# Diagonals, means and the own norm placed anew around the layer norms of a two-block layer on one Trainium2 core

## The chip, the cores and the metric

One core of a Trainium2 chip runs the whole program. The metric is device microseconds of one execution. TensorE is called PE, VectorE DVE, ScalarE ACT, GpSimd POOL and SyncE, which issues the DMAs, SP.

## What is computed

x is 1024 tokens by 1024 features. A first block (gated linear attention, cross attention, an output product) is followed by a second one, of which the change touches the conformer convolution and what stands beside it:

```python
hl = modulate(rms_norm_2(xl, norm1_g[i]), sh1_l, s1_l)
yl = conformer_conv(hl, rows, *conv_p)
xl = xl + g1_l * yl
xl = xl + g2_l * sq_relu_mlp(modulate(rms_norm_2(xl, norm2_g[i]), sh2_l, s2_l), mlp_w1[i], mlp_w2[i])
...
def conformer_conv(h, n_seg, w_pw1, b_pw1, w_dw, b_dw, ln_g, ln_b, w_pw2, b_pw2):
    u = h @ w_pw1 + b_pw1
    a, gate = jnp.split(u, 2, axis=-1)
    u = a * jax.nn.sigmoid(gate)
    u = dwconv(u.reshape(B * n_seg, L // n_seg, D), w_dw).reshape(B, L, D) + b_dw
    u = jax.nn.silu(layer_norm(u, ln_g, ln_b))
    return u @ w_pw2 + b_pw2
```

The convolution is depthwise with 31 taps in segments of 64 tokens. The first block ends in an rms norm of its own (`final_norm_w`), whose result is the xl above.

## The kernel before

Features lie on partitions (8 tiles f or k of 128), tokens along the free dimension, in two halves h of 512. Every product is done in three matmuls per k and 512 tokens (weights high x data high, high x low, low x high, line 1133), called a group here; a product of 1024 inputs for one f and one h has 8 groups. Weights come as units of 128 x 1024 into a ring of four slots: SP loads a unit, ACT (line 1507) makes its high part WH, POOL (line 2320) its low part WL.

`make_plan` (line 143) writes one order of pieces, by a small model of time: `tick` advances PE's time at each group and lets lanes of DVE and POOL work run until they are `AHEAD` (2.5 us) ahead of it, and lets background generators (`bg`) take a step. Each engine's program then walks through the plan and issues, in that order, what its piece means for it; each engine works strictly in order and waits on semaphores.

Half by half the second block does this. `between_blocks(h)` makes the norms and the modulated input (`m1_mul`, `m1_hi`, `m1_lo`, the tile HB). For each f the products `pa(f,h)` and `pg(f,h)` are gated (`glu`: ACT's sigmoid at line 1714, DVE's product into a padded tile UP). Then comes the convolution: on DVE for six of the f (`tap` x 31 into the banks 4 and 5, `taps_end`, result CO for half 0, COB for half 1), for f 1 and 5 on ACT and POOL (`ptap`, lines 1738 and 2362). There are ten UP tiles, so the products of half 1 run up to f 7 while half 0 is convolved.

The layer norm of a half is `means` (a matmul of ones with each CO[f], line 1390, added up over f in one bank), then `normed`: `ysub` on DVE (CO less the mean), `ysq` on ACT (the square, tile YT), `ysum` on PE (four matmuls with one column of ones, each in two passes, line 1398), `ln_r` (DVE, POOL's power, DVE's diagonal LNDG), `ln_row` (a matmul that spreads the diagonal over the partitions, line 1373), and `z_mul`, `z_hi`, `z_lo`, the input of the second pointwise product `pw2`. The own norm of the first block is `own_norm(h)`: the diagonal DGR (DVE, line 2170), the row from it (PE, line 1373), and `pre` (DVE line 2179, ACT line 1722) for eight f, on the residual RES. `pw2` outputs are added to RES, which is why `pre(f,h)` must be done by then.

Half 0's layer norm stands alone (`beside(normed(0), ...)`): nothing else is there for PE. Half 1's (`conv_norm(1)`) runs as background beside the first groups of the MLP of half 0. After `pw2` of half 0 follow its squares (`sq`, `sq_add`, tile ACC), `n3_sum`, `n3_row`, the modulation `m2_*` and the MLP (`hid`, `w2_out`).

Of the kernel before, what the change touches and what calls it, by code (L numbers as in the profile page):

```python
# [142 lines left out]
def make_plan():  # L143
# [8 lines left out]
    hi_by = ["act"]  # L152
# [463 lines left out]
    co_done = set()  # L616
    rate[0] = 1.0

    def conv_dve(f, h):
        for k in range(TAPS):  # L620
            piece("tap", f, h, k)
            yield
        piece("taps_end", f, h)
        co_done.add((f, h))
        up_free[(8 * h + f) % 10] = True
        yield

    def conv_pool(f, h):
        piece("ptap0", f, h)
        for k in range(1, TAPS):  # L630
            piece("ptap", f, h, k)
            yield
        co_done.add((f, h))
        up_free[(8 * h + f) % 10] = True
# [26 lines left out]
    def means(h):  # L661
        take(S, "mean", h)
        for f in range(8):
            while (f, h) not in co_done:
                yield
            piece("mean", f, h)
            now["pe"] += 4 * PASS
            yield

    def normed(h):  # L670
        take(S, "ysum", h)
        for f in range(8):
# [4 lines left out]
            yield  # L677
        piece("ysum", 7, h)
# [24 lines left out]
    for h in range(2):  # L703
        for f in range(8):
# [3 lines left out]
            product("pa", f, h)  # L708
            product("pg", f, h)
# [25 lines left out]
    beside(normed(0), {7: 3, 8: 1, 9: 2, 10: 1})  # L735
# [6 lines left out]
    def second_product(h):  # L742
# [128 lines left out]
def build_program(nc, wall, wmod, xT, memT, vecs, gup, ident_d, masks_d, out, oscr):  # L871
    es = ExitStack()
    with es:
# [142 lines left out]
        YT = [[at(f"YT{h}{i}", 512, F32, x0 + (10, 18)[h] * K2 + i * K2) for i in range(2)] for h in range(2)]  # L1016
        LNDG = [at(f"LNDG{h}", 512, F32, x0 + (12, 20)[h] * K2) for h in range(2)]
# [75 lines left out]
        def pe_program(pe):  # L1093
# [409 lines left out]
        def act_program(ac):  # L1503
# [236 lines left out]
            def ysq(f, h):  # L1740
# [56 lines left out]
        def dve_program(dv):  # L1797
# [367 lines left out]
            def r1_row(h):  # L2165
# [4 lines left out]
                tt(*spread_of(DGR[:, :], hs(R1, h), 4), ALU.mult).then_inc(sig["r1_row"], 1)  # L2170
# [98 lines left out]
            def final(h, k):  # L2269
# [12 lines left out]
                        r1_row=r1_row, pre=pre, ysub=ysub, ln_r=ln_r, z_mul=z_mul, z_lo=z_lo, gbv=gbv, a2=a2, pw2=pw2, n3_sum=n3_sum, n3_row=n3_row, hid=hid,  # L2282
# [272 lines left out]
```

## Time and profile before

| | us |
|---|---|
| runs | 2236.50, 2244.32, 2230.09; median 2236.5 |
| profiled execution | 2237.09 |
| its span in the profile | 2235.3 |
| PE busy | 2081.1 (93%) |
| DVE busy | 1185.3 (53%) |
| ACT busy | 676.6 (30%) |
| POOL busy | 867.3 (39%) |

The convolution of half 0 with its products runs from about 1144 to 1345 us of the span, the layer norm of half 0 from 1345 to 1379, `pw2` and the norm behind it to 1445, the MLP of half 0 with the convolution of half 1 beside it to about 1623. Busy time is that of the data paths; an engine that waits on a semaphore is idle. The idle time given with a row is what stood before it, and the name behind the arrow is who ended it.

### The profile page before, as it was taken

What the parts mean: (1) busy time and instruction counts of PE and PEld (TensorE: products, weight loads), DVE (VectorE), ACT (ScalarE), POOL (GpSimd) and SP (SyncE); (2) the same over time, 40 slices, a digit from 0 to 9 for tenths busy, and PEclk for the clock granted to TensorE, in tenths of its full rate; (3) what the DMA queues carried; (4) which work ended last, traced back from release to release, by engine and by line L of the source; (5) the groups of instructions that cost most, each with busy time, mean ns of one, the idle gap of its engine ahead of it and who ended that gap; (6) DMA issues with size and microseconds to landing.
All of it is one profiled execution on the core that took longest, in us unless ns stands there. A gap on an engine that the chain in (4) does not pass through costs nothing.

```text
span 2235.3 us, 26278 instructions
## 1 busy us (share of the span) xinstructions
PE 2081.1 (93%) x10286; PEld 1730.9 (77%) x10286; DVE 1185.3 (53%) x1977; ACT 676.6 (30%) x1200; POOL 867.3 (39%) x511
## 2 busy tenths in 40 slices
PE   6899999898998989999979977879999999999997
PEld 5779988787887768888858766658778888888886
DVE  5353455365463346776677967979735222222226
ACT  2313222211136411010345435465434322212111
POOL 7342122221111344453438872679444442222120
PEclk9999999999899999999989997889999999999998
DMA  4211011101010454454113221123223332111112
GB/s 160 67 48 57 29 39 57 38 34 35 27 34 34 140 193 157 149 183 140 40 46 97 93 67 47 57 66 94 72 89 95 94 96 65 57 48 53 51 48 76
DMA packets 57323, 171.59 MB, mean 77 GB/s; under 512 B 6368, under 2 KB 6752, under 8 KB 57072
## 3 DMA queue, kind: packets, MB, share of 16 engines
q1 hardware_dynamic: 57200, 169.91, 23.4%
q8 instruction: 82, 1.34, 0.2%
q14 instruction: 41, 0.34, 0.0%
HBM read 157.30 MB, written 12.58 MB: 76 GB/s over the span
## 4 chain that ended last, share of the span: by engine, by line
PE 78%; DVE 11%; issue 4%; ACT 4%; POOL 2%; DMA 1%; SPq 0%; POOLq 0%; DVEq 0%; ACTq 0%
PE B L1133 37%; PE B L1316 22%; PE B L1199 6%; PE B L1237 4%; DVE B L1804 3%; DVE OSB L1807 1%; DMA MODRAW<-wmod 1%; POOL WL L2320 1%; DVE HB L1804 1%; PE B L1261 1%; DVE ACC L1801 1%; PE B L1264 1%; PE B L1398 1%; PE B L1277 1%; PE B L1373 1%
## 5 line engine op out<-in xcount | busy, mean ns | idle before, releaser
L1133 PE MATMUL B<-HB,WH 128*128 128x512 f32 x2976 | 947.2, 406 | 29.3 <-ACT WH L1507 13.5
L2320 POOL TENSOR_TENSOR WL<-RAW,WH 128x1024 fp32r<-128x1024 f32 x217 | 529.0, 2441 | 531.8 <-ACT WH L1507 525.4
L1133 PEld LDWEIGHTS B<-HB,WH 128*128 128x128 f32 x2976 | 558.8, 192 | 158.6 <-issue 32.3
L1133 PE MATMUL B<-HB,WL 128*128 128x512 f32 x1488 | 569.1, 396 | 7.2 <-POOL WL L2320 7.2
L1133 PEld LDWEIGHTS B<-HB,WL 128*128 128x128 f32 x1488 | 285.0, 192 | 71.1 <-POOL WL L2320 10.1
L1804 DVE SCALAR_TENSOR_TENSOR B<-UP,vec,B 128x512 f32<-128x512 f32 x336 | 226.6, 748 | 0.0
L1804 DVE SCALAR_TENSOR_TENSOR RES<-B,modv,RES 128x512 f32<-128x512 f32 x144 | 104.9, 747 | 195.2 <-PE B L1316 164.9
L1507 ACT ACTIVATE WH<-RAW 128x1024 fp32r<-128x1024 f32 x144 | 150.7, 1053 | 161.9 <-DMA RAW<-wall 161.9
L2318 POOL TENSOR_SCALAR WH<-RAW 128x1024 fp32r<-128x1024 f32 x73 | 85.5, 1171 | 286.6 <-DMA RAW<-wall 286.6
L2297 POOL TENSOR_TENSOR small<-small 128x4 f32<-128x4 f32 (+2 forms) x36 | 36.7, 1019 | 403.3 <-DVE small L1807 403.2
L1316 PE MATMUL B<-HIDH,WH 128*128 128x512 f32 x512 | 185.3, 395 | 0.0
L1316 PE MATMUL B<-HIDL,WH 128*128 128x512 f32 x512 | 182.9, 390 | 0.0
L1316 PE MATMUL B<-HIDH,WL 128*128 128x512 f32 x512 | 182.8, 390 | 0.0
L1199 PE MATMUL B<-WH,HB 128*128 128x256 f32 x768 | 147.4, 293 | 0.0
L1804 DVE SCALAR_TENSOR_TENSOR B<-B,RL 128x512 f32<-128x512 f32 x64 | 44.5, 696 | 190.0 <-ACT RL L1774 189.8
L1199 PEld LDWEIGHTS B<-WH,HB 128*128 128x128 f32 x768 | 122.5, 194 | 3.1 <-issue 1.5
L1804 DVE SCALAR_TENSOR_TENSOR MACC<-MODRAW,small,MACC 128x512 f32<-128x512 f32 x84 | 102.3, 1218 | 35.3 <-DMA MODRAW<-wmod 29.8
L1316 PEld LDWEIGHTS B<-HIDL,WH 128*128 128x128 f32 x512 | 96.6, 189 | 20.4 <-issue 0.7
L1316 PEld LDWEIGHTS B<-HIDH,WH 128*128 128x128 f32 x512 | 96.6, 189 | 20.3 <-issue 0.7
L1316 PEld LDWEIGHTS B<-HIDH,WL 128*128 128x128 f32 x512 | 96.5, 189 | 20.2
L1199 PE MATMUL B<-WL,HB 128*128 128x256 f32 x384 | 109.4, 285 | 0.0
L1738 ACT ACTIVATE PR<-UP,vec 128x512 f32<-128x512 f32 x120 | 84.5, 723 | 53.7 <-POOL COB L2362 32.5
(235 smaller groups left out, 2734.3 us busy)
## 6 DMA issues: line engine op xcount, KB each, us to landing
RAW<-wall SPq DMA_DIRECT2D x217, 512.0 KB, 3.5
MODRAW<-wmod SPq DMA_DIRECT2D x96, 256.0 KB, 2.7
RES<-xT SPq DMA_DIRECT2D x16, 512.0 KB, 6.8
oscr<-OT SPq DMA_DIRECT2D x32, 256.0 KB, 2.0
OI<-oscr SPq DMA_DIRECT2D x16, 512.0 KB, 3.3
outT<-RES SPq DMA_DIRECT2D x16, 256.0 KB, 2.1
mraw<-memT SPq DMA_DIRECT2D x1, 1024.0 KB, 13.7
mst<-masks SPq DMA_DIRECT2D x1, 224.0 KB, 14.7
```

Source lines behind the costliest of these rows:

```text
L1133: i = pe.matmul(bank, a[:, ks], hb(part, k, h), start=k == 0 and n == 0, stop=k == 7 and n == 2)
L1199: i = pe.matmul(bank[:, tl * 256:(tl + 1) * 256], hb(part, k)[:, t * 128:(t + 1) * 128], b[:, k % 4 * 256:(k % 4 + 1) * 256], start=k == 0 ...
L1237: i = pe.matmul(bank[0:m, c % 4 * 64:c % 4 * 64 + 64], ch(k, c)[:, 0:m], odd, start=True, stop=True)
L1261: pe.matmul(bank[:, 0:dv], ch(KT_, c), vc, start=True, stop=True).then_inc(done, 1)
L1264: i = pe.matmul(bank[:, 0:dv], ch(AB, c), vc, start=True, stop=c == 0)
L1316: i = pe.matmul(bank, a[:, ks], rhs(part, h), start=k == 0 and n == 0, stop=k == 3 and n == 2)
L1507: return ac.activation(o, i, ACT.Copy, **kw)
L1738: ac.activation(seg(PR[n % 2][:, :]), tap(f, h, k), ACT.Copy, scale=wcol(f, k)).then_inc(sig["ptap_act"], 1)
L1804: return dv.scalar_tensor_tensor(out=o, in0=a, scalar=s, in1=b, op0=op0, op1=op1)
L2297: po.tensor_tensor(o, o, mhalf[:, 0:n], ALU.pow).then_inc(sig[made], 1)
L2318: po.tensor_scalar(hi, raw, 1.0, 0.0, ALU.mult, ALU.add).then_inc(sig[f"w_hi{q % NW}"], 1)
L2320: po.tensor_tensor(lo, raw, hi.bitcast(F32), ALU.subtract).then_inc(sig[f"w_lo{q % NW}"], 1)
```

## The change

1. `r1_row` is split. The diagonal is a piece of its own, `r1_dg`, and the row a later one. In half 0 the diagonal is made where it was, and the row and the eight `pre` move from the third product into `normed(0)`, between `ysum(6,0)` and `ysum(7,0)`; the row takes a bank of the ring B in place of S. In half 1 eight background steps lie between diagonal and row.
2. `means` adds the f in the order in which the model of time has them done, each only when PE's time is `LATE` (8 us) past that, or when all are done.
3. The first `pa` and `pg` are done side by side, group by group.
4. The last `pw2` of a half lets the DVE and POOL lanes run only up to PE's time (`ahead[0] = 0.0`).
5. Four tiles YT for the squares in place of two; their places in memory and those of LNDG, SQ3, TN and DG3 move.

```diff
+LATE = 8.0
...
-            while lanes[lane] and now[lane] < now["pe"] + AHEAD:
+            while lanes[lane] and now[lane] < now["pe"] + ahead[0]:
...
     def own_norm(h):
 
+        piece("r1_dg", h)
+        for _ in range(8):
+            yield
         take(S, "r1_row", h)
         piece("r1_row", h)
...
     def means(h):
+
         take(S, "mean", h)
-        for f in range(8):
-            while (f, h) not in co_done:
-                yield
-            piece("mean", f, h)
-            now["pe"] += 4 * PASS
+        left = list(range(8))
+        while left:
+            ready = [f for f in left if (f, h) in co_done and (now["pe"] > co_done[f, h] + LATE or len(co_done) == 8 + 8 * h)]
+            if ready:
+                f = min(ready, key=lambda f: co_done[f, h])
+                left.remove(f)
+                piece("mean", f, h, len(left))
+                now["pe"] += 4 * PASS
             yield
...
+        if h == 0:
+            take(B, "r1_row", 0)
+            piece("r1_row", 0)
+            for f in range(8):
+                piece("pre", f, 0)
         piece("ysum", 7, h)
...
-            product("pa", f, h)
-            product("pg", f, h)
+            if f == 0 and h == 0:
+                names = [("pa", 0, 0), ("pg", 0, 0)]
+                together(names, names)
+            else:
+                product("pa", f, h)
+                product("pg", f, h)
...
-                bg.append(own_norm(0))
+                piece("r1_dg", 0)
...
-    beside(normed(0), {7: 3, 8: 1, 9: 2, 10: 1})
+    beside(normed(0), {9: 2, 10: 1})
...
+            if f == 7:
+                ahead[0] = 0.0
             product("pw2", f, h)
             done(f)
+        ahead[0] = AHEAD
...
-                if f >= 2:
-                    w.wait_ge(sig["ysum"], nth["ysum", f - 2, h] - h)
-                ac.activation(YT[h][f % 2][:, :], CO[h][f][:, :], ACT.Square).then_inc(sig["ysq"], 1)
+                if f >= 4:
+                    w.wait_ge(sig["ysum"], nth["ysum", f - 4, h] - h)
+                ac.activation(YT[h][f % 4][:, :], CO[h][f][:, :], ACT.Square).then_inc(sig["ysq"], 1)
```

The order that comes out differs as follows. On PE, at the first groups of `pa(2,0)` (bank B0; B3 is the end of `pg(1,0)`), before:

```order
L1133 MATMUL B3<-HB_49,WL_51 128x512
L1133 MATMUL B0<-HB_49,WH_50 128x512 x2
L1133 MATMUL B0<-HB_49,WL_51 128x512
L1373 MATMUL B6<-DGR_166,ones_54 128x512
L1133 MATMUL B0<-HB_49,WH_50 128x512 x2
L1133 MATMUL B0<-HB_49,WL_51 128x512
```

and now:

```order
L1153 MATMUL B3<-HB_49,WL_51 128x512
L1153 MATMUL B0<-HB_49,WH_50 128x512 x2
L1153 MATMUL B0<-HB_49,WL_51 128x512
L1153 MATMUL B0<-HB_49,WH_50 128x512 x2
L1153 MATMUL B0<-HB_49,WL_51 128x512
L1153 MATMUL B0<-HB_49,WH_50 128x512 x2
```

The row from DGR has left the product; the groups around it are the same.

On DVE, at the end of the convolution of half 0 (UP7 is the input of f 7, UP8 that of f 0 of half 1, UP5 the gating of `(7,1)`, CO0 the first `ysub`), before:

```order
L1804 SCALAR_TENSOR_TENSOR UP5_159<-B2,vec_56,SG1_129 128x8x64
L1804 SCALAR_TENSOR_TENSOR B5<-UP7_161,vec_56,B5 128x512
L1804 SCALAR_TENSOR_TENSOR B4<-UP7_161,vec_56,B4 128x512
L1804 SCALAR_TENSOR_TENSOR B5<-UP7_161,vec_56,B5 128x512
L1804 SCALAR_TENSOR_TENSOR CO7_137<-UP7_161,vec_56,B4 128x512
L1801 TENSOR_TENSOR CO7_137<-CO7_137,B5 128x512
L1804 SCALAR_TENSOR_TENSOR CO0_130<-B7,CO0_130 128x512
```

and now:

```order
L1824 SCALAR_TENSOR_TENSOR CO7_137<-UP7_165,vec_56,B4 128x512
L1821 TENSOR_TENSOR CO7_137<-CO7_137,B5 128x512
L1827 TENSOR_SCALAR B4<-UP8_166,vec_56 128x512
L1827 TENSOR_SCALAR B5<-UP8_166,vec_56 128x512
L1824 SCALAR_TENSOR_TENSOR B4<-UP8_166,vec_56,B4 128x512
L1824 SCALAR_TENSOR_TENSOR B5<-UP8_166,vec_56,B5 128x512
L1824 SCALAR_TENSOR_TENSOR B4<-UP8_166,vec_56,B4 128x512
L1824 SCALAR_TENSOR_TENSOR UP5_163<-B2,vec_56,SG1_129 128x8x64
L1824 SCALAR_TENSOR_TENSOR CO0_130<-B6,CO0_130 128x512
```

The taps and the end of f 7 and five taps of half 1 have gone ahead of the last gating, which the first `ysub` now follows directly. On PE the last pair of products, `pa(7,1)` and `pg(7,1)`, had `mean(5)` after one group, `mean(6)` after three and `mean(7)` behind it; now it has `mean(7)` after one group and `mean(5)` after three.

On PE, at the end of the layer norm of half 0 (YT the squares, DGR the own norm's diagonal, LNDG the layer norm's), before:

```order
L1398 MATMUL B6<-ones_54,YT01_147 128x1 x4
L1398 MATMUL B6<-ones_54,YT00_146 128x1 x4
L1398 MATMUL B6<-ones_54,YT01_147 128x1 x4
L1398 MATMUL B6<-ones_54,YT00_146 128x1 x4
L1398 MATMUL B6<-ones_54,YT01_147 128x1 x4
L1373 MATMUL B7<-LNDG0_150,ones_54 128x512
L1133 MATMUL B0<-HB_49,WH_50 128x512 x2
```

and now:

```order
L1418 MATMUL B7<-ones_54,YT03_149 128x1 x4
L1418 MATMUL B7<-ones_54,YT00_146 128x1 x4
L1418 MATMUL B7<-ones_54,YT01_147 128x1 x4
L1418 MATMUL B7<-ones_54,YT02_148 128x1 x4
L1393 MATMUL B0<-DGR_170,ones_54 128x512
L1418 MATMUL B7<-ones_54,YT03_149 128x1 x4
L1393 MATMUL B6<-LNDG0_154,ones_54 128x512
L1153 MATMUL B1<-HB_49,WH_50 128x512 x2
```

The row of the own norm stands ahead of the last sum. On DVE its eight `pre` follow the last `ysub` and stand ahead of `ln_r`, whose two instructions came there behind three taps.

In `pw2` of half 0 six taps stood ahead of the last output on DVE, and two do now. In half 1 the row from DGR stood on PE behind the first group of `hid(4)`, and stands now behind the fifth of `hid(5)`, 12 groups later; the diagonal stays behind `hid(3)` on DVE. The eight `pre` of half 1 stood there around `hid(4)` and stand now around `hid(6)`.

## Rows read from the trace of the kernel before

**Rows 1.** Busy time of each engine by stretch, us; PEclk: the granted clock.

```profile
core 0: us, PE busy (x) PEld busy (x) DVE busy (x) ACT busy (x) POOL busy (x), PEclk, DMA share, GB/s
...
1168.00:1314.00 146.00, 146.00 (x634) 119.01 (x633) 122.80 (x184) 72.50 (x97) 125.86 (x78) 1.00 0.29 91
...
1348.00:1363.00 15.00, 13.79 (x64) 13.73 (x64) 6.11 (x11) 6.06 (x9) 0.39 (x1) 0.50 0.00 1
...
1500.00:1600.00 100.00, 99.09 (x445) 80.40 (x443) 86.75 (x132) 47.24 (x66) 75.57 (x44) 1.00 0.29 90
1600.00:1681.00 81.00, 77.75 (x348) 63.08 (x348) 35.67 (x51) 32.05 (x43) 31.08 (x15) 0.98 0.26 80
```

**Rows 2.** PE's waits by line and releaser: us in all, times, longest.

```profile
PE B L1373 <- DVE DGR L1801: 16.4, 2, 9.3
...
PE B L1390 <- POOL CO L2362: 11.9, 1, 11.9
PE B L1352 <- DVE ACC L1801: 8.7, 3, 5.6
```

**Rows 3.** Timeline of PE at `pa(2,0)`: start, us, operation, idle time before.

```profile
1165.96 2.05 PE L1373 MATMUL B<-DGR,ones 128*128 128x512 f32 x2 [9.34 <-DVE DGR L1801]
```

**Rows 4.** Timeline of DVE, own norm and first gatings of half 0.

```profile
1168.05 5.36 DVE L1804 SCALAR_TENSOR_TENSOR RES<-RES,vec,B 128x512 f32<-128x512 f32 x8 [2.23 <-PE B L1373]
...
1190.39 0.76 DVE L1804 SCALAR_TENSOR_TENSOR UP<-B,vec,SG 128x512 f32<-128x512 f32 x1 [5.51 <-ACT SG L1714]
1191.06 8.65 DVE L1804 SCALAR_TENSOR_TENSOR B<-UP,vec,B 128x512 f32<-128x512 f32 x13
1201.27 0.75 DVE L1804 SCALAR_TENSOR_TENSOR UP<-B,vec,SG 128x512 f32<-128x512 f32 x1 [1.56 <-ACT SG L1714]
```

**Rows 5.** Timeline of POOL: splits of weights, and the last adds of the convolution.

```profile
1165.55 2.48 POOL L2320 TENSOR_TENSOR WL<-RAW,WH 128x1024 fp32r<-128x1024 f32 x1 [12.37 <-ACT WH L1507]
...
1173.55 2.40 POOL L2320 TENSOR_TENSOR WL<-RAW,WH 128x1024 fp32r<-128x1024 f32 x1
...
1315.15 11.13 POOL L2362 TENSOR_TENSOR CO<-CO,PR 128x512 f32<-128x512 f32 x8 [1.74 <-ACT PR L1738]
```

**Rows 6.** Timeline of PE at the means of half 0.

```profile
1326.34 2.08 PE L1390 MATMUL B<-CO,ones 128*128 128x512 f32 x2 [11.93 <-POOL CO L2362]
...
1344.93 2.08 PE L1390 MATMUL B<-CO,ones 128*128 128x512 f32 x2 [4.97 <-DVE CO L1801]
```

**Rows 7.** Timeline of DVE, end of the convolution and layer norm of half 0.

```profile
1314.56 0.75 DVE L1804 SCALAR_TENSOR_TENSOR UP<-B,vec,SG 128x512 f32<-128x512 f32 x1 [0.79 <-ACT SG L1714]
...
1340.77 0.75 DVE L1804 SCALAR_TENSOR_TENSOR UP<-B,vec,SG 128x512 f32<-128x512 f32 x1 [14.92 <-issue]
...
1344.19 0.69 DVE L1801 TENSOR_TENSOR CO<-CO,B 128x512 f32<-128x512 f32 x1
1347.04 4.87 DVE L1804 SCALAR_TENSOR_TENSOR CO<-B,CO 128x512 f32<-128x512 f32 x8 [2.17 <-PE B L1390]
...
1362.37 0.16 DVE L1807 TENSOR_SCALAR small<-B 128x4 f32<-128x4 f32 x1 [8.42 <-PE B L1398]
```

**Rows 8.** Groups of PE and ACT by line, from 1348 to 1363 us.

```profile
L1398 PE MATMUL B<-ones,YT 128*128 128x1 f32 x64 | 13.8, 352 | 1.5 <-ACT YT L1751 1.5
...
L1751 ACT ACTIVATE YT<-CO 128x512 f32<-128x512 f32 x8 | 5.0, 630 | 14.0 <-DVE CO L1804 7.1 <-PE B L1398 6.9
```

**Rows 9.** Timeline of PE: a column sum of the first block's norm.

```profile
1131.65 0.95 PE L1352 MATMUL B<-ones,ACC 128*128 128x1 f32 x8
```

**Rows 10.** Timelines of DVE and PE at the end of `pw2` of half 0.

```profile
1418.62 4.03 DVE L1804 SCALAR_TENSOR_TENSOR B<-UP,vec,B 128x512 f32<-128x512 f32 x6
...
1425.64 1.87 PE L1352 MATMUL B<-ones,ACC 128*128 128x1 f32 x8 [5.65 <-DVE ACC L1801]
```

**Rows 11.** Timelines of DVE and PE at the own norm of half 1.

```profile
1471.29 0.68 DVE L1801 TENSOR_TENSOR DGR<-ident,small 128x512 f32<-128x512 f32 x1
...
1472.12 2.05 PE L1373 MATMUL B<-DGR,ones 128*128 128x512 f32 x2 [7.08 <-DVE DGR L1801]
```

More of the change, by code:

```diff
@@ L151, in make_plan @@
     lanes = {"dve": [], "pool": []}
-    hi_by = ["act"]
+    hi_by, ahead = ["act"], [AHEAD]
     def u_split():
@@ L615, in make_plan @@
     up_free = [True] * 10
-    co_done = set()
+    co_done = {}
     rate[0] = 1.0
@@ L623, in conv_dve @@
         piece("taps_end", f, h)
-        co_done.add((f, h))
+        co_done[f, h] = now["dve"]
         up_free[(8 * h + f) % 10] = True
@@ L632, in conv_pool @@
             yield
-        co_done.add((f, h))
+        co_done[f, h] = now["pool"]
         up_free[(8 * h + f) % 10] = True
@@ L1015, in build_program @@
               [at(f"COB{f}", 512, F32, hb0 + (8 + f) * K4 + K2) for f in range(8)]]
[L1016 to L1017 removed]
+        YT = [[at(f"YT{h}{i}", 512, F32, x0 + (10, 18)[h] * K2 + i * K2) for i in range(4)] for h in range(2)]
+        LNDG = [at(f"LNDG{h}", 512, F32, x0 + (14, 22)[h] * K2) for h in range(2)]
         RL = at("RL", 512, F32, x0 + 16 * K2)
@@ L1384, in r1_row, with mean @@
             def r1_row(h):
-                row(("r1_row", h), DGR[:, :], "r1_row")
-            def mean(f, h):
-                bank, done = start(("mean", h), f == 0)
+                row(("r1_row", h), DGR[:, :], "r1_dg")
+            def mean(f, h, left):
+                bank, done = start(("mean", h), left == 7)
                 conv_done(w, f, h)
-                i = pe.matmul(bank, ones[:, :], CO[h][f][:, :], start=f == 0, stop=f == 7)
-                if f == 7:
+                i = pe.matmul(bank, ones[:, :], CO[h][f][:, :], start=left == 7, stop=left == 0)
+                if left == 0:
                     i.then_inc(done, 1)
@@ L1397, in ysum @@
                 for t in range(4):
-                    i = pe.matmul(bank[:, t:t + 1], YT[h][f % 2][:, t * 128:(t + 1) * 128], ones[:, 0:1],
+                    i = pe.matmul(bank[:, t:t + 1], YT[h][f % 4][:, t * 128:(t + 1) * 128], ones[:, 0:1],
                                   start=f == 0 and t == 0, stop=f == 7, skip_group_check=True)
@@ L2163, in taps_end, with r1_dg @@
                 tt(co, co, BANKS[5], ALU.add).then_inc(sig["taps_end"], 1)
-            def r1_row(h):
+            def r1_dg(h):
                 w.wait_ge(sig["n1_pow"], 2 * h + 1)
@@ L2169, in r1_row @@
                     wait_full(w, "r1_row", 0)
-                tt(*spread_of(DGR[:, :], hs(R1, h), 4), ALU.mult).then_inc(sig["r1_row"], 1)
+                tt(*spread_of(DGR[:, :], hs(R1, h), 4), ALU.mult).then_inc(sig["r1_dg"], 1)
             def pre(f, h):
@@ L2281, in dve_program @@
                         m1_lo=m1_lo, m2_mul=m2_mul, m2_lo=m2_lo, glu=glu, tap=tap_, taps_end=taps_end,
-                        r1_row=r1_row, pre=pre, ysub=ysub, ln_r=ln_r, z_mul=z_mul, z_lo=z_lo, gbv=gbv, a2=a2, pw2=pw2, n3_sum=n3_sum, n3_row=n3_row, hid=hid,
+                        r1_dg=r1_dg, pre=pre, ysub=ysub, ln_r=ln_r, z_mul=z_mul, z_lo=z_lo, gbv=gbv, a2=a2, pw2=pw2, n3_sum=n3_sum, n3_row=n3_row, hid=hid,
                         w2_out=w2_out, n4_sum=n4_sum, n4_row=n4_row, final=final)
```

6 lines of the change are left out of this document (3 added, 3 removed).

## The prediction, made before the changed kernel was run

> **What bounds the kernel now.** I read first the busy shares, then the waits of TensorE (PE), then the timelines of its neighbours around each wait that the change touches. PE is the engine to follow: from 1168 to 1314 us it is busy without a gap, and from 1500 to 1681 us nearly so [rows 1]. So time is won only where PE stands still, and every microsecond won there moves all that follows. Its long waits near the change are few [rows 2]: 16.4 us in two waits for DGR, the diagonal of the own norm; 11.9 us for CO from GpSimd (POOL), a mean that isn't ready; and the waits for sums of squares (ACC), 5.6 us of them at the end of the second pointwise product of half 0. Besides these there is the layer norm of half 0: PE is busy in it, but with one-column matmuls at a granted clock of 0.50 [rows 1, 8], and the whole chain behind it waits.
>
> **Half 0, the row taken out of the third product (+8.4, later +7.4).** PE ended a group of `pa(2,0)` at 1156.62 and stood 9.34 us until DGR was made [rows 3]. DVE made DGR only after the whole modulation of half 1. Now the product goes on. Two products of eight groups take 1201.27 - 1190.39 = 10.88 us [rows 4], 0.68 a group. The 15 groups left of `pa(2,0)` and `pg(2,0)` end at 1156.4 + 15 x 0.68 = 1166.6. Then a new wait: the low part of the next weights is POOL's, whose split starts at 1165.55 as before, since ScalarE (ACT) reaches its half of it only behind the modulation; it is done at 1168.0, so `pa(3,0)` ends near 1173.4. The split after it comes behind four adds of the convolution and ends at 1173.55 + 2.40 = 1175.95 [rows 5]; nothing of the change moves it. So `pg(3,0)` ends at 1175.95 + 5.1 = 1181.0. Before it ended about 1.0 us ahead of the gating at 1190.39, at 1189.4. Of 10.4 us freed (the wait, and about 1.1 for the row), 8.4 are kept. From there POOL's two splits and four adds a pair (2 x 2.40 + 4 x 1.39 = 10.4 us, [rows 5]) stay below the 10.88 of PE, so the lead holds. DVE has its eight own-norm rows (5.36 us, [rows 4]) taken away and 13 to 15 taps of 0.665 us (8.65 / 13, [rows 4]) per pair: it keeps up. By the gating of `(6,1)` one more mean has been placed on PE; two passes cost 2.08 us at the low clock [rows 6], about 1.0 at the high one. So that gating moves from 1314.56 [rows 7] to 1307.2. Bounds: 4 (a third weight wait) to 10.4.
>
> `pa(0,0)` and `pg(0,0)` side by side I cost at nothing: PE then has more to do while DVE delivers k by k, but the same seven groups stand behind the sum of squares of half 1, which waits for DVE's ACC in either order. Freed slots come 10 us later for one weight load, and its split is needed only 10 us after that. Bounds -1 to +2.
>
> **Half 0, means by completion (+9.3).** Before, PE met `mean(5)` after one group of the last pair, waited 11.93 us for POOL, and the gating `(7,1)` fell at 1340.77; DVE stood 14.9 us for it with 4 taps of `(7,0)` to go, ended them at 1344.88 and subtracted the mean from 1347.04 [rows 6, 7]. Now DVE finishes `(7,0)` in front of that gating: 1307.2 + 0.7 + 10 x 0.665 + 0.7 = 1315.2. PE meets `mean(7)` near 1307 and waits 8 us for it, in place of 11.9 and 5.0. `mean(5)` is ready by then: POOL's last eight adds took 11.13 us from 1315.15 [rows 5]; seven, 7.4 us earlier, end at 1317.5. What follows the first of two means was 15.1 us before (1326.34 to the end of the gating, 1341.43; [rows 6, 7]) and consists of the same groups now. So the subtraction starts at 1330.3 in place of 1347.04: 16.7 in all, 7.4 + 9.3. The new chain is convolution, mean, product, gating, subtraction; before, the product lay beside it. Bounds 5 to 12.
>
> **Half 0, layer norm (-4.0).** Two buffers of squares never held PE: its 64 one-column matmuls run 13.79 us without a gap, 1.72 us for each f, while ACT, at 0.63 a square, waits for PE [rows 8]. Four buffers shorten nothing there. But `r1_row` now stands ahead of the last column sum on PE (2.08 us at the low clock), and DVE has eight rows of `pre` (5.36 us) queued ahead of `ln_r`. With the clock low throughout: the first sum starts 1.5 us after the subtraction, seven sums 12.0, the row 2.1, `pre` 5.4: 21.0 us from subtraction to `ln_r`, where 1362.37 - 1347.04 = 15.3 stood [rows 7]. That costs 5.7. What they hide in is only the last 1.7 us sum. If the clock stayed high, a sum would cost 0.95 (eight such matmuls at 1131.65, [rows 9]) and the total would be 1.5 + 6.6 + 1.1 + 5.4 = 14.6, a gain of 0.7. PE comes to it after ten busy microseconds and a stand of 3 us, so I let two sums run fast: -4.0. Bounds -5.7 and +0.7. ACT's eight `pre` follow DVE's one by one, and the row of the norm behind `ln_r` covers the last of them.
>
> The Trainium skill (TensorE: Matmul & The Clock Gate, Part 1, "What's actually happening") says that the throttled clock is the default and that activity releases it. Read simply, gapless PE should be given its full clock; the row at 0.50 speaks against that for one-column matmuls. By the rule the layer norm would gain 0.7 instead of losing 4.0 and the sum would be 27.2; that is rival B.
>
> **Half 0, fewer taps ahead of the last output (+2.4).** Six taps ran in front of the last `pw2` output, 1418.62 to 1422.65, while PE had ended at 1425.64 - 5.65 = 1419.99 [rows 10]. Two taps end at 1419.95. The four moved ones are made up before `hid(0)`, where DVE bounds: both orders have 23 taps from the row of n3 to there, so the 2.4 stays. Bounds 0 to 2.5.
>
> **Half 1, diagonal ahead of its row (+7.4).** PE stood 7.08 us for DGR, with one group of `hid(4)` done, and ran the row at the low clock [rows 11]. Now 12 groups lie between; DGR, made at 1471.97, is ready when the row is reached near 1475. 7.1 are saved, 1.0 more from the clock, and 0.7 given back where the mean of f 7 and the first square meet PE late. From 1500 to 1600 us DVE is busy 86.75 and POOL 75.57 of 100 us [rows 1]: following 7 us faster uses most of DVE's room, so I bound it by 1.5 (DVE becomes the bound) and 9. Behind it PE is busy to the end and nothing gives the lead back.
>
> Sum: 7.4 + 9.3 - 4.0 + 2.4 + 7.4 = 22.5. Against the profiled execution's 2237.1 (span 2235.3 and 1.8 around it) that is 2214.6; this execution is 0.6 above the median of the runs, 2236.5, from which I go: **2214.0 us**. About 1%, 22.4 us, is what a measurement of this kernel can tell from no change; the forecast sits on that line.
>
> **Rivals.**
> A, the forecast: 0.55, own range 2209 to 2219.
> B, the layer norm at the high clock: 2214.0 - 4.7 = 2209.3. For it: 0.95 us a sum after busy PE. Against: 13.79 us at 0.50. 0.08.
> C, half 1 isn't kept: DVE or POOL can't follow, and PE waits again for a bank or weights: 7.4 becomes 1.5, 2219.9. For it: DVE 87% busy. Against: 13 us in 100 are idle there [rows 1]. 0.17.
> D, the lead of the first product is eaten by weights: ACT and POOL serve splits between taps in a fixed order; 8.4 becomes 3.4: 2219.0. For it: two new waits already in my count. Against: the cadence, 10.4 below 10.88. 0.13.
> E, slower: the last product of half 0 now stands behind `mean(7)`. Should the taps of `(7,0)` end where they did (1344.88), because DVE and not PE paces them, the subtraction starts at 1344.88 + 15.1 = 1360.0, 13.0 late; with -4.0, +2.4 and +7.4 the kernel takes 7.2 more: 2243.7. It decides from an end of taps past 1315.2 + 22.5 = 1337.7. Against: DVE idled ahead of each gating shown (5.51, 1.56, 0.79 us, [rows 4, 7]). 0.07.
> That the change doesn't do what it says is open for the four buffers alone, and is in A.
>
> **How the numbers follow.** The range 2206 to 2226 takes in A with its bounds, B, C and D; E is outside. Faster by over 1% (below 2214.1): half of A's 0.55, B, and some of the upper bounds of C and D: 0.45. Slower by over 1% wants E worse than worked out, or two losses at once: 0.04. The rest, 0.51, is within 1%.
>
> **What would show it.** In the changed profile: no DGR among PE's waits; the pair of f 3 gated at about 1182; a wait of 7 to 9 us for CO7 from DVE and none from POOL; subtraction near 1330; PE's one-column run with a row in it, DVE's `ln_r` 19 to 21 us behind the first subtraction; the ACC wait near 3.2 us; no new PE wait after 1450. A first subtraction later than 1338 breaks the second term, a PE wait for weights or banks between 1460 and 1600 the last one, and a clock of 1.0 in the sums the third.

## The result: 2216.0 us, and half of the terms moved elsewhere

| | before | changed |
|---|---|---|
| median | 2241.1 us (5 runs, 2230.1 to 2244.3) | 2216.0 us (5 runs, 2214.1 to 2221.6) |
| ratio | | 0.9902, 95% interval 0.9873 to 0.9932 |
| span of the profiled execution | 2235.3 us | 2214.2 us |

The prediction said 2214.0 us, 22.5 us saved; the spans differ by 21.1, the medians by 25.1, since the two further runs of the kernel before moved its median from 2236.5 to 2241.1. The total came out, but not by the sum that was written down: one term was half due to another cause than the one named, one loss was taken too small, and one gain was won in full and then mostly lost to a wait that the prediction had not seen. The waits of the matrix engine in the changed kernel (line and releaser, us in all, times, longest):

```profile
PE B L1153 <- POOL WL L2340: 10.1, 7, 2.2
...
PE B L1410 <- DVE CO L1821: 8.3, 1, 8.3
...
PE B L1393 <- DVE LNDG L1821: 5.9, 1, 5.9
...
PE B L1153 <- issue: 4.9, 1, 4.9
...
PE B L1418 <- ACT YT L1771: 3.8, 2, 3.0
```

DGR (16.4 us in [rows 2]) is gone, and so is the mean of POOL (11.9). The wait for CO from DVE is 8.3 us, as forecast, where 5.0 stood [rows 6]; LNDG has 5.9 us, where 3.0 stood in two waits; and new are 4.9 us with "issue" as releaser: nothing that the profile could name.

DVE in half 0 (start, us, operation, idle time before it), to be laid beside [rows 4, 7]: the gating of f 3, that of `(6,1)`, the end of f 7, the last gating, the first subtraction, the eight `pre`, and `ln_r`:

```profile
1181.62 0.75 DVE L1824 SCALAR_TENSOR_TENSOR UP<-B,vec,SG 128x512 f32<-128x512 f32 x1
...
1304.52 0.75 DVE L1824 SCALAR_TENSOR_TENSOR UP<-B,vec,SG 128x512 f32<-128x512 f32 x1 [1.15 <-ACT SG L1734]
...
1311.89 0.69 DVE L1821 TENSOR_TENSOR CO<-CO,B 128x512 f32<-128x512 f32 x1
...
1327.19 0.75 DVE L1824 SCALAR_TENSOR_TENSOR UP<-B,vec,SG 128x512 f32<-128x512 f32 x1 [11.26 <-issue]
1327.86 4.86 DVE L1824 SCALAR_TENSOR_TENSOR CO<-B,CO 128x512 f32<-128x512 f32 x8
1343.30 5.36 DVE L1824 SCALAR_TENSOR_TENSOR RES<-RES,vec,B 128x512 f32<-128x512 f32 x8 [10.58 <-PE B L1393]
1348.57 0.15 DVE L1827 TENSOR_SCALAR small<-B 128x4 f32<-128x4 f32 x1
```

The gating of f 3 moved from 1190.39 to 1181.62, that of `(6,1)` from 1314.56 to 1304.52, the subtraction from 1347.04 to 1327.86. But `ln_r` is 20.7 us behind the subtraction, where it was 15.3.

PE in the same stretch: the wait for f 7, the mean of f 5, seven column sums, the own norm's row, the eighth sum, the layer norm's row:

```profile
1312.63 2.08 PE L1410 MATMUL B<-CO,ones 128*128 128x512 f32 x2 [8.26 <-DVE CO L1821]
...
1316.49 1.02 PE L1410 MATMUL B<-CO,ones 128*128 128x512 f32 x2
...
1329.34 12.00 PE L1418 MATMUL B<-ones,YT 128*128 128x1 f32 x56 [2.97 <-ACT YT L1771]
1341.21 2.05 PE L1393 MATMUL B<-DGR,ones 128*128 128x512 f32 x2
1343.05 1.71 PE L1418 MATMUL B<-ones,YT 128*128 128x1 f32 x8
1350.69 2.05 PE L1393 MATMUL B<-LNDG,ones 128*128 128x512 f32 x2 [5.93 <-DVE LNDG L1821]
```

Further on, the sum of squares behind `pw2` of half 0, the row from DGR of half 1, which waits for nothing now, and the first group of `pw2(0,1)`:

```profile
1409.77 1.05 PE L1372 MATMUL B<-ones,ACC 128*128 128x1 f32 x8 [3.60 <-DVE ACC L1821]
...
1458.27 1.02 PE L1393 MATMUL B<-DGR,ones 128*128 128x512 f32 x2
```

```profile
1589.69 1.02 PE L1393 MATMUL B<-LNDG,ones 128*128 128x512 f32 x2
...
1598.15 0.74 DVE L1824 SCALAR_TENSOR_TENSOR RES<-B,modv,RES 128x512 f32<-128x512 f32 x1
...
1601.02 0.69 DVE L1821 TENSOR_TENSOR HB<-COB,HB 128x512 fp32r<-128x512 f32 x1 [0.34 <-ACT HB L1527]
1601.63 0.75 DVE L1824 SCALAR_TENSOR_TENSOR RES<-B,modv,RES 128x512 f32<-128x512 f32 x1
...
1602.29 0.68 DVE L1821 TENSOR_TENSOR COB<-COB,B 128x512 f32<-128x512 f32 x1
...
1602.48 1.19 PE L1153 MATMUL B<-HB,WH 128*128 128x512 f32 x2 [4.93 <-issue]
```

In the last fence PE starts `pw2(0,1)` at 1602.48 after 4.93 us, 0.10 us behind the end of a DVE instruction (1601.63 + 0.75) that adds an output to RES. That is the epilogue of a `w2_out`, and it stands in DVE's queue behind the layer norm's subtractions. What that means, e5 and e8 settle.

**A ladder.** Totals of single executions of one kernel spread over 10 to 15 us, and the first gating, ahead of which nearly nothing was edited, fell anywhere from 1139.7 to 1148.9 us in these runs. So the parts are read from one table, made from the timelines of each profiled execution. Its columns are the distances between: the first gating `(0,0)` on DVE; the gating `(6,1)`; the first subtraction of half 0; LNDG of half 0 on DVE; the layer norm's row of half 1 on PE; the first group of `pw2(0,1)`.

| | to gating (6,1) | to subtraction | to LNDG | to row, half 1 | to pw2(0,1) | sum |
|---|---|---|---|---|---|---|
| before | 170.5 | 32.5 | 16.6 | 247.9 | 11.9 | 479.3 |
| changed | 162.2 | 23.3 | 22.0 | 239.8 | 12.8 | 460.2 |
| e1 | 163.8 | 23.2 | 22.1 | 239.4 | 17.2 | 465.8 |
| e2 | 162.3 | 23.3 | 22.0 | 241.3 | 15.7 | 464.5 |
| e3 | 161.3 | 18.7 | 16.6 | 244.7 | 3.7 | 445.0 |
| e4 | 163.9 | 11.8 | 21.1 | 243.1 | 8.3 | 448.1 |
| e5 | 164.0 | 24.8 | 20.6 | 239.6 | 7.7 | 456.7 |
| e6 | 161.8 | 28.1 | 22.1 | 239.3 | 7.7 | 458.9 |
| e7 | 161.4 | 18.7 | 16.6 | 244.8 | 3.7 | 445.2 |
| e8 | 171.6 | 33.0 | 16.6 | 248.3 | 17.2 | 486.7 |
| e9 | 164.0 | 11.8 | 12.8 | 247.5 | 3.5 | 439.5 |
| e10 | 162.2 | 23.4 | 22.0 | 247.0 | 7.7 | 462.3 |
| e11 | 163.1 | 24.7 | 20.7 | 239.3 | 7.7 | 455.5 |

The changed kernel, e1, e2, e5, e10 and e11 run the same order from the gating of f 1 to LNDG, but for the buffers in e11. Their distances scatter over 162.2 to 164.0, 23.2 to 24.8 and 20.6 to 22.1: 1.5 to 2 us is what this table can tell in each of its first three columns.

Most of this scatter is PE's granted clock. Some 31 us behind the first gating PE ends its wait of 2.1 us for weights. In the changed kernel, e2 and e10 it goes on at 1.00 and the first column is 162.2; in e1 and e5 it is granted 0.50 for some 3 us, and the column is 163.8 and 164.0 (so too in e4 and e9). The stretch behind that wait, the changed kernel first, then e5:

```profile
1173.00:1177.00 4.00, 3.66 (x16) 3.05 (x17) 4.00 (x7) 1.97 (x4) 3.86 (x4) 1.00 0.13 51
...
1171.00:1175.00 4.00, 3.78 (x10) 2.97 (x11) 4.00 (x8) 1.98 (x4) 3.86 (x4) 0.57 0.15 61
```

(PEclk is the third number from the end.) In e11 the clock is 1.00 there, and the 0.9 us over 162.2 stand between its first two gatings. Behind the wait for CO the clock comes back to 1.00 later in e5 and e11 than in the other four, which gives 24.8 and 24.7 in the second column; these two then run the start of the column sums at 1.00, which gives 20.6 and 20.7 in the third. Both columns together are 45.3 to 45.4 us in all six runs, so from the gating `(6,1)` to LNDG the table can tell differences of well under 1 us. Why the same order is granted one clock in one execution and the other in the next is not shown.

Of the 21.1 us of span, 1.8 are ahead of the first gating, 19.1 are in the table and 0.2 behind it.

### The profile page after: what moved, and what is told of

Same layout as the page of the kernel before. It is cut to its first block, busy times and chain, and to the rows that moved or that the text cites. A ratio compares the mean times of both kernels' runs of the same rounds, so it can differ in the third digit from the quotient of the medians.

```text
span 2214.2 us, 26275 instructions
## 1 busy us (share of the span) xinstructions
PE 2074.0 (94%) x10286; PEld 1728.3 (78%) x10286; DVE 1173.6 (53%) x1977; ACT 675.7 (31%) x1200; POOL 867.5 (39%) x511
## 4 chain that ended last, share of the span: by engine, by line
PE 79%; DVE 10%; issue 4%; ACT 3%; POOL 2%; DMA 1%; SPq 0%; POOLq 0%; DVEq 0%; ACTq 0%
PE B L1153 38%; PE B L1336 23%; PE B L1219 6%; PE B L1257 4%; DVE B L1824 2%; POOL WL L2340 1%; DVE OSB L1827 1%; DMA MODRAW<-wmod 1%; DVE HB L1824 1%; DVE ACC L1821 1%; PE B L1418 1%; PE B L1281 1%; PE B L1284 1%; PE B L1297 1%; DVE RES L1824 1%
```

## The experiments

Every ratio is against the kernel before, with its 95% interval. The first question was the 4.93 us at `pw2(0,1)`: theory G, stated with e1, held that PE waits there for its input from the layer norm.

### e1: the last pw2 with the lanes ahead again

```diff
-            if f == 7:
-                ahead[0] = 0.0
```

> The changed kernel with edit 4 taken back: DVE and POOL may run 2.5 us ahead through the last pw2 too. Theory G (groups): in half 1, pw2 starts when its input from the layer norm is there, some 12.8 us behind the row of the layer norm, and PE has in that time 0.45 us for the row and 0.74 us for each group of w2_out that the plan puts between the two. Edit 4 left 10 such groups where before had 16, since the planner's DVE lane stands later; with it taken back 16 stand there again. So the 4.93 us wait of PE ahead of pw2(0,1) goes to 0 to 0.5, and the wait for ACC at the end of pw2 of half 0 comes back from 3.60 to about 5.65: +2.1, and up to 0.8 more by the clock of the sum. Sum: 1.5 to 2.5 us faster than the changed kernel, span about 2212.5. Theory P (the prediction's step): edit 4 is a gain of 2.4 us alone, the wait of 4.93 us is DVE's convolution or another of the parts and stays: span 2216.6.

Measured: 0.9945 (0.9923 to 0.9967), above the changed kernel's 0.9902 (0.9873 to 0.9932), with intervals that just overlap. PE's wait for ACC at the end of `pw2` is back, and so is the low clock of the sum behind it:

```profile
1420.04 1.87 PE L1370 MATMUL B<-ones,ACC 128*128 128x1 f32 x8 [5.71 <-DVE ACC L1819]
```

That is 5.71 us in place of 3.60 and a sum of 1.87 in place of 1.05; from LNDG to the row behind this sum it is 2.9 us. So edit 4 is worth 2.1 us, forecast 2.4, and 0.8 by the clock in this pair of runs. But theory G fell: 16 groups stand ahead of `pw2(0,1)` here, and PE still waited 5.22 us. Here too it begins 0.1 us behind an epilogue (1613.84 + 0.74):

```profile
1613.84 0.74 DVE L1822 SCALAR_TENSOR_TENSOR RES<-B,modv,RES 128x512 f32<-128x512 f32 x1
...
1614.69 1.19 PE L1151 MATMUL B<-HB,WH 128*128 128x512 f32 x2 [5.22 <-issue]
```

### e2: the means of half 1 in the fixed order

```diff
+            if h:
+                ready = [f for f in left[:1] if (f, h) in co_done]
+            else:
+                ready = [f for f in left if (f, h) in co_done and ...]
```

> The changed kernel with the means of half 1 added in the fixed order and without LATE, as before the change; half 0 as changed. 13 groups of w2_out then stand between the row of the layer norm of half 1 and pw2, where 10 stand in the changed kernel. Theory G: the wait ahead of pw2(0,1) is 12.8 - 0.45 - 13 x 0.74 = 2.7 us in place of 4.93, span 2212.0. Theory D: the taps of half 1 on DVE and POOL set the end of the means; then an earlier mean(7,1) waits for COB, and what is won at pw2 is lost there: no change of the span, 2214.2, and a wait of about 2 us for COB.

Measured: 0.9943 (0.9921 to 0.9965). The wait at `pw2(0,1)` is 5.72 us, not the 2.7 of theory G. The wait for COB of theory D is there, 1.8 us, but its balance isn't. From LNDG to `pw2(0,1)` it takes 257.0 us, where the changed kernel takes 252.6. So the order by completion with LATE is worth some 4 us in half 1, as long as the wait at its end stands. Theory G is out: 13 groups or 16, the wait stays at 5 us.

### e3: the own norm's row and pre out of the layer norm

```diff
-                piece("r1_dg", 0)
+                bg.append(own_norm(0))
...
-        if h == 0:
-            take(B, "r1_row", 0)
-            piece("r1_row", 0)
-            for f in range(8):
-                piece("pre", f, 0)
```

The background step waits 12 steps between diagonal and row in half 0, so that no wait for DGR returns; the row takes a bank of S again.

> The changed kernel with the own norm's row and its eight pre of half 0 taken out of the layer norm: the row stands in pa(3,0), 12 steps behind the diagonal, and the eight pre beside the taps. If the row and pre cost the layer norm what the trace says (20.71 us from the first subtraction to ln_r, 15.33 before), that stretch is 15.3 us and 5.4 us are won there, with no wait for DGR. If instead the sums' low clock or the gating set it, it stays above 18. The plan then leaves only 4 groups of w2_out between the row of the layer norm of half 1 and pw2: by theory G the wait there grows from 4.93 to 9.4 us, so of 5.4 only 1.0 is left: span about 2213. Without theory G: span 2208.8.

Measured: 0.9845 (0.9816 to 0.9875), 11 us better than the changed kernel by the medians and much more than expected. From subtraction to LNDG it is 16.6 us, to the hundredth as before the change, so the layer norm's loss of 5.4 us was the row and the `pre`. The wait that theory G made 9.4 us was none at all. And the subtraction came 4.7 us sooner behind the gating `(6,1)`, because the planner, with its DVE lane later, now put the last means behind the product. Three effects, two of them not meant; e4 and e5 take them apart.

### e4: the last means behind the product

```diff
-... or len(co_done) == 8 + 8 * h)]
+... or closed[0] and len(co_done) == 8 + 8 * h)]
...
+    closed[0] = True
     while bg:
         step_in(bg)
```

`closed[0]` is False until the sixteen products and the taps of half 0 are planned.

> The changed kernel with the last two means of half 0 (f 7 and 5) behind pg(7,1) in place of inside pa(7,1). Theory: in the changed kernel PE stands 8.26 us for CO7 with 15 groups of product queued behind the mean, so convolution, mean, product, gating, subtraction form one chain. With the means behind the product, PE runs the product beside the last taps, ends it near 1315, and the first subtraction starts at about 1319 in place of 1327.9: 8 to 9 us earlier. 7 groups are left ahead of pw2 in half 1 (theory G: wait 7.2 us in place of 4.93, -2.3). Span about 2208. Rival: POOL's mean of f 5 isn't there before 1325, and less than 3 us are won: span 2213 or more.

Measured: 0.984 (0.9805 to 0.9874). From the gating `(6,1)` to the subtraction it takes 11.8 us in place of 23.3. PE doesn't wait for CO: the means of f 7 and 5 run in one piece behind the product, and DVE, which ended f 7 at 1319.3, stood 0.21 us ahead of the last gating.

```profile
1321.10 1.88 PE L1412 MATMUL B<-CO,ones 128*128 128x512 f32 x4
```

```profile
1318.58 0.69 DVE L1823 TENSOR_TENSOR CO<-CO,B 128x512 f32<-128x512 f32 x1
...
1322.17 0.75 DVE L1826 SCALAR_TENSOR_TENSOR UP<-B,vec,SG 128x512 f32<-128x512 f32 x1 [0.21 <-issue]
1323.02 4.87 DVE L1826 SCALAR_TENSOR_TENSOR CO<-B,CO 128x512 f32<-128x512 f32 x8
```

So the chain of convolution, mean, product, gating and subtraction, which the prediction had described and priced only as a rival's danger, cost 11.5 us in this column. Counted from the first gating to LNDG it is 10.8 us (207.6 to 196.7), since e4 had the low clock at the weight wait.

### e5 and e8: the ring of banks, from both sides

```diff
-    B = Ring([0, 1, 2, 3, 4, 5])
+    B = Ring([1, 2, 3, 0, 4, 5])      (e5, the changed kernel)
+    B = Ring([3, 0, 1, 2, 4, 5])      (e8, the kernel before)
```

> The changed kernel with one line edited: the ring of six banks from which pw2 of half 1 takes begins with 1, 2, 3, 0 in place of 0, 1, 2, 3. Theory R (ring): in the changed kernel the own norm's row takes a bank of ring B, which turns the ring by one for all that follows; so pw2(0,1) writes bank 0, which the last output in front of it, w2_out(2,7,0), still holds, and its epilogue on DVE stands behind the subtractions z of the layer norm. In every run so far in which PE stood there, it began 0.1 us behind such an epilogue (1602.38 to 1602.48 in the changed kernel). With the ring begun at 1 the bank's epilogue is four outputs old: no wait, pw2(0,1) starts 4 to 4.9 us earlier, span about 2209.5 for a run that comes there as the changed kernel did. Theory G (the input from the layer norm isn't there) is weak after e1 and e2, where 16 and 13 groups changed nothing (waits of 5.22 and 5.72 us): by it the wait stays near 4.9 and the span at 2214.

> The kernel before with one line edited: the ring of six banks begins with 3, 0, 1, 2 in place of 0, 1, 2, 3, so that pw2(0,1) writes bank 3, which w2_out(2,7,0) still holds. Nothing else of the change is in it. Theory R: PE came to pw2(0,1) at 1623.41 there, and the epilogue of that output ended at 1628.7; so a wait of 5.2 us appears and the kernel is 4 to 5 us slower than before (ratio 1.002). Without theory R: no wait, ratio 1.000.

Measured, e5: 0.9889 (0.9859 to 0.9919), span 2207.5; e8: 1.0036 (1.0014 to 1.0058). In e5 PE begins `pw2(0,1)` 7.70 us behind the layer norm's row, where the changed kernel took 12.79, with no wait:

```profile
1589.02 1.02 PE L1393 MATMUL B<-LNDG,ones 128*128 128x512 f32 x2
...
1596.72 0.62 PE L1153 MATMUL B<-HB,WH 128*128 128x512 f32 x2
...
1597.47 0.74 DVE L1824 SCALAR_TENSOR_TENSOR RES<-B,modv,RES 128x512 f32<-128x512 f32 x1
```

An epilogue still comes at 1597.47, but PE writes another bank and doesn't mind it. In e8, with nothing of the change in it, the wait is there:

```profile
1626.81 0.74 DVE L1804 SCALAR_TENSOR_TENSOR RES<-B,modv,RES 128x512 f32<-128x512 f32 x1
...
1627.65 1.19 PE L1133 MATMUL B<-HB,WH 128*128 128x512 f32 x2 [5.19 <-issue]
```

5.19 us with the releaser "issue", 0.10 us behind an epilogue's end, as in the changed kernel; of the 7.4 us that e8's ladder is longer than that of the kernel before, 5.3 are in this last column. One line made it and one line removed it, so this is shown (by the traces: the intervals of the totals of e5 and of the changed kernel overlap): the own norm's row, taken from ring B in edit 1, turned the ring by one; at the switch from four banks to six, `pw2(0,1)` then met the bank of the very last `w2_out`.

### e6: the means of half 0 in the fixed order, on e5

```diff
+            if not h:
+                ready = [f for f in left[:1] if (f, h) in co_done]
```

> e5 with the means of half 0 in the fixed order of before (mean(5), mean(6), mean(7) inside pa(7,1)). By the prediction's second term the order by completion is worth 9.3 us: span of e5 plus 9. By the trace of the changed kernel POOL's CO5 is done at 1314.85, 2.2 us behind the mean(7) that PE waits for, and one more mean (1.0 us) would stand between: the first subtraction comes 3 us later than in e5, since the taps of f 7 stay in front of the last gating in either. Then most of the 9.1 us isn't the order of the means but the taps of f 7, which end earlier because the eight pre of the own norm no longer stand among them.

Measured: 0.9903 (0.9874 to 0.9932) beside e5's 0.9889. PE waits for POOL's mean of f 5 again, 11.94 us:

```profile
1313.23 2.07 PE L1413 MATMUL B<-CO,ones 128*128 128x512 f32 x2 [11.94 <-POOL CO L2385]
...
1317.24 1.02 PE L1413 MATMUL B<-CO,ones 128*128 128x512 f32 x2
...
1318.79 1.02 PE L1413 MATMUL B<-CO,ones 128*128 128x512 f32 x2
```

And yet from the gating `(6,1)` to LNDG it takes 50.1 us, where the six runs of the order by completion took 45.3 to 45.4. From the first gating, where one mean less stands ahead of `(6,1)` and the clock scatters, it is 211.9 beside 207.5 to 209.3. The order by completion is worth 3 to 5 us, not 9.3.

### e7: e3 and e4 together

Both diffs above.

> e3 and e4 together: row and eight pre of half 0's own norm out of the layer norm (the row in a bank of S again, so that ring B isn't turned), and the means of f 5 and 7 behind pg(7,1). Counted from the first gating: first subtraction 9 to 10 us ahead of the changed kernel's, the layer norm 5.4 us shorter (15.3 us from subtraction to ln_r), no wait for a bank at pw2(0,1) (4.9): 19 to 20 us in all, span about 2195 (2192 to 2199). If the two overlap (both move the last means), the first subtraction gains no more than 9.9, and the sum is unchanged. Rival: with the eight pre among the taps again DVE ends f 7 later and the subtraction gains under 7: span 2198 or more.

Measured: 0.9863 (0.9832 to 0.9894), no better than e3 or e4 alone; the rival held. The means had been behind the product in e3 already, and with the `pre` among the taps DVE ends f 7 at 1321.3, 4.1 us behind the last gating's start, so that the subtraction waits for the taps (PE's wait of 3.42 us for CO in the last fence of this document). What is won in the layer norm by moving the `pre` is paid at the end of the convolution.

### e9: the row in PE's gap, the pre behind the layer norm

```diff
         take(S, "ysum", h)
+        if h == 0:
+            take(B, "r1_row", 0)
+            piece("r1_row", 0)
         for f in range(8):
             piece("ysub", f, h)
...
-        if h == 0:
-            take(B, "r1_row", 0)
-            piece("r1_row", 0)
-            for f in range(8):
-                piece("pre", f, 0)
...
+    bg.append(pres())
     second_product(0)
```

`pres()` gives one `pre` a step. The means are as in e4, the ring as in e5.

> e4 (means of f 5 and 7 behind pg(7,1)) with the ring of e5, the own norm's row of half 0 on PE between the last mean and the first column sum, and its eight pre behind the last z, beside pw2. PE stood 1.5 to 3.0 us between last mean and first sum, and the row takes 2.05 us there. Theory: the first subtraction stays where e4 has it, 175.7 + 1000 us behind the first gating's zero, that is 175.7 us behind the first gating; the layer norm, subtraction to LNDG, takes 16.6 us (as before and in e3 and e7) in place of 21.07; pw2(0,1) has no wait for a bank (2.43 in e4). So pw2(0,1) starts 441 us behind the first gating, where the changed kernel has 460.2, e4 448.1 and e7 445.2; span 4 us under e7's, about 2198. Rival: the eight pre (5.36 us) push the taps and outputs of pw2 on DVE and the wait for ACC at its end grows from 3.6 to over 7 us: then no better than e7, span 2202 or more.

Measured: median 2199.3 us, 0.9838 (0.9808 to 0.9868), 16.7 us under the changed kernel's median and some 14 by the two ratios. By its interval it can't be told from e3 or e4. By the ladder it is the shortest, 439.5 us, 20.7 under the changed kernel and 5.4 under e3. The wait for ACC stayed at 3.6 us. Not all was kept: from LNDG to `pw2(0,1)` it takes 251.0 us, 3.7 more than in e5. In `pw2` PE waits 0.87 us for RES, which the late `pre` write, and at `pw2(0,1)` it waits 2.38 us for HB from ACT, its input from the layer norm of half 1: what theory G had named is real here, where the row of that layer norm is followed by `pw2` after 3.5 us. The layer norm is 12.8 us, 3.8 shorter than before the change and than the theory said:

```profile
1322.73 1.88 PE L1416 MATMUL B<-CO,ones 128*128 128x512 f32 x4
1324.45 1.02 PE L1399 MATMUL B<-DGR,ones 128*128 128x512 f32 x2
1326.15 9.95 PE L1424 MATMUL B<-ones,YT 128*128 128x1 f32 x64 [0.68 <-ACT YT L1777]
1338.26 2.05 PE L1399 MATMUL B<-LNDG,ones 128*128 128x512 f32 x2 [2.17 <-DVE LNDG L1827]
```

The row went into the gap, and the 64 one-column matmuls took 9.95 us in place of 13.79 [rows 8]. The granted clock tells why (columns as in [rows 1]): 1.00 in their first four microseconds, 0.50 later. In e4, with the same means and no row in the gap, it was 1.00 for little more than the first microsecond, and the 64 took 12.77 us (11.06 and 1.71). One profile of each is on record.

```profile
core 0: us, PE busy (x) PEld busy (x) DVE busy (x) ACT busy (x) POOL busy (x), PEclk, DMA share, GB/s
...
1326.00:1330.00 4.00, 3.85 (x35) 3.88 (x35) 3.52 (x6) 3.68 (x8) 2.01 (x1) 1.00 0.00 0
1331.00:1336.00 5.00, 5.00 (x24) 5.00 (x24) 0.00 (x0) 0.88 (x1) 0.00 (x0) 0.50 0.01 2
```

### e10: the row of half 1 back behind its diagonal, on e5

```diff
         piece("r1_dg", h)
-        for _ in range(8):
-            yield
         take(S, "r1_row", h)
```

> e5 with the eight steps between diagonal and row of half 1 taken out, so that the row from DGR follows the first group of hid(4) again, as before the change. The prediction's last term: PE waits 7.1 us for DGR again, and 1 us more by the clock, less 0.7; all of it reaches the end, since nothing else held half 1 but the ring. Span of e5 plus 7.4, pw2(0,1) 464 us behind the first gating where e5 has 456.7. Rival: half 1 is held by DVE's taps behind it, and 3 us or less of the wait reach pw2(0,1).

Measured: 0.9923 (0.99 to 0.9945), and the wait is back at its old size:

```profile
1460.13 2.04 PE L1391 MATMUL B<-DGR,ones 128*128 128x512 f32 x2 [7.08 <-DVE DGR L1819]
```

From LNDG of half 0 to the layer norm's row of half 1 it takes 247.0 us in place of e5's 239.6: 7.4, the prediction's figure. Behind that row both take 7.7.

### e11: two buffers of squares, pa and pg apart, on e5

```diff
-                names = [("pa", 0, 0), ("pg", 0, 0)]
...
-                if f >= 4:
-                    w.wait_ge(sig["ysum"], nth["ysum", f - 4, h] - h)
-                ac.activation(YT[h][f % 4][:, :], ...)
+                if f >= 2:
+                    w.wait_ge(sig["ysum"], nth["ysum", f - 2, h] - h)
+                ac.activation(YT[h][f % 2][:, :], ...)
```

> e5 with two parts taken back that the prediction costed at nothing: two tiles YT for the squares in place of four, and pa(0,0) ahead of pg(0,0) in place of side by side. Prediction: no change within 1 us, the 64 one-column matmuls of half 0 run without a gap in 13.8 us. Rival: two tiles hold the sums of half 1, which run at the high clock (0.95 us for eight), and the row of its layer norm comes later; or the products apart save a wait for weights at pg(2,0) (2.17 us in the changed kernel).

Measured: 0.9899 (0.9864 to 0.9934), e5 0.9889; the ladder's sum is 455.5 beside 456.7. The second to fifth columns agree within 0.4 us, so the buffers do nothing, as costed. In the first, e11 had the high clock at the weight wait and e5 the low one: beside the 162.2 of the three runs with the high clock e11 is 0.9 later, all of it between the first two gatings. That is inside the -1 to +2 of the prediction, and one trace isn't enough to call it a cost.

## Why the prediction was right, and where it was right by luck

**First term, the third product (7.4).** Right. 8.2 us were won from the first gating to `(6,1)`. The two new waits for POOL's low part are there, 0.89 and 2.17 us at 1165.44 and 1173.34, and the gating of f 3 fell at 1181.62, forecast 1182. That closeness is luck in part: 1.8 us of it were there at the first gating already. Counted from there, f 3 came 7.0 us sooner (46.3 to 39.3), not 8.4, because DVE ran 13 taps straight up to this gating: it was DVE and not PE that set it, against "it keeps up". By f 6 the lead was 9.1. And in the four runs with the low clock behind the second of these waits the term would have been 6.5 to 6.7.

**Second term, means by completion (9.3).** The size held: 9.1 us from `(6,1)` to the subtraction. PE's wait for CO7 is 8.26 us, forecast 8. But the step that named the cause held only in part: the order of the means is worth 3 to 5 us (e6). Some 4.4 more (32.5 to 28.1) are there in e6 too, with the old order. What carried them is that DVE ends f 7 ahead of the last gating, in either order, since the eight `pre` are no longer among its taps; e3 and e7, where they are and f 7 ends behind that gating, point to the same, but no run moves the `pre` alone. The prediction had put the tap order into its sum, but under the heading of the means. And it took the chain through the product for the price of the edit, while e4 shows that it was 11.5 us lying there for a condition of one word.

**Third term, the layer norm (-4.0).** The mechanism was right, the size wrong: -5.4 (16.6 to 22.0). The step that failed is "two sums run fast". PE had a granted clock of 1.00 up to 1329 and 0.50 from 1330, and the seven sums took 12.00 us. The worked-out figure for a clock low throughout, -5.7, was the better one. e3 and e7, at 16.62 and 16.61, show that nothing but the row and the `pre` made it. With the same order e5 and e11 had the start of the sums at 1.00 and lost 4.0 and 4.1 us, the forecast figure; what they gained there they had lost in the column before.

The Trainium skill (TensorE: Matmul & The Clock Gate, Part 1, "What's actually happening") says that the throttled clock is the default and that activity releases it. e9 doesn't agree with it in that simple form: PE was busy without a gap from 1331 to 1336 and was granted 0.50, having had 1.00 before. The measurement decides.

**Fourth term, fewer taps ahead of the last output (2.4).** Right: 2.05 us less of waiting for ACC, which e1 gave back; 0.8 more came by the clock of the sum behind it, which was not forecast and isn't there in every run (1.86 us for this sum in e3, behind a wait of 3.53).

**Fifth term, half 1 (7.4).** The term itself is exact, 7.4 in e10. The statement "no new PE wait after 1450" failed. The step that failed is one that is missing: point 1 of the change says that the row takes a bank of the ring B in place of S, and the prediction gives that no price, as if a bank of a ring were a matter of its moment only. It turned the ring for the rest of the kernel and cost 4.9 us 260 us later. About 1.3 us came back: waits for COB and LNDG in half 1 vanished (0.35, 0.76 and 0.84 in the trace of before), and one for YT grew from 0.15 to 0.84. Rival C had the place and a price (5.9 of 7.4 lost) but another cause, a DVE or POOL that can't follow; neither bounded anything there.

**Sum.** 8.2 + 9.1 - 5.4 + 8.0 - 0.9 = 19.1 in the ladder, forecast 22.5, with 1.8 us ahead of the first gating that belong to no edit. So the closeness of 2214.0 and 2216.0 overstates the prediction: without the turned ring the kernel takes 2209.8 us (e5), 4 less than forecast.

Rival D is out: of the first lead nothing is eaten by `(6,1)`. Rival E is out by 25 us: the taps of f 7 ended at 1312.6, it decides from 1337.7.

What stays open: why the first gating itself falls up to 9 us apart, why the same order is granted a different clock from one execution to the next, and whether e9 is better than e3 and e4 by total time; its advantage is shown in the ladder alone.

## What to carry to other kernels

When an instruction moves and takes its buffer from a rotating pool, follow the pool to its next irregular point (a switch of size, another user): a wait that appears far behind with no releaser in the profile, and ends just as another engine's epilogue does, may be a turned ring, and one line tests it. A small reduction whose input comes late should not stand inside a long product on an engine that works in order: put it behind, and the product covers the wait. And what moves out of one engine's queue (here the eight `pre`) has to be followed to where it lands, since the layer norm and the convolution's end each paid for it, and beside `pw2` it cost PE one wait of 0.87 us. And before a difference of 1 to 2 us between two traces is given to an edit, the granted clock behind each wait should be laid side by side.

## What the runs showed of the hardware

PE's granted clock falls while PE issues one-column matmuls without a gap: 64 of them behind busy products and one row took 9.95 us (e9), with the clock falling to 0.50 after 4 us; behind the same products without the row 12.77 us (e4), with the clock falling after 1 us; and 13.78 us where the clock was 0.50 already, behind a wait of 3.42 us and one mean (e7). Eight of them between groups of a product took 0.95 us in half 1. So the row in the gap of 1.5 us cost PE nothing, and the run of 64 was 2.8 us shorter than in e4. The moment of the fall scatters by some 1.5 us between runs of one order (the changed kernel and e5), so of the 2.8 us not all need be the row's.

```profile
1321.36 2.07 PE L1407 MATMUL B<-CO,ones 128*128 128x512 f32 x2 [3.42 <-DVE CO L1818]
1324.97 13.78 PE L1415 MATMUL B<-ones,YT 128*128 128x1 f32 x64 [1.54 <-ACT YT L1768]
```

The clock also decides small things elsewhere: the sum of squares behind `pw2` took 1.87 us behind a wait of 5.71 us (e1). Behind waits of 3.5 to 3.8 us it took 1.05 in the changed kernel, e2, e5, e10 and e11, but 1.41 in e9, 1.77 in e4 and 1.86 in e3. So the length of the wait alone doesn't decide it.
